# Differential heads' norm factors: one transposition to rows, a store to DRAM and four loads into all partitions, in place of sixteen transpositions

## The chip, the cores and the metric

The kernel runs on one core of a Trainium2 chip. The metric is the device time of one execution in microseconds (us), the median over the runs. TensorE is called PE in the profile, its weight loads PEld, VectorE DVE, ScalarE ACT, GpSimd POOL and SyncE SP.

## The reference, cut to what matters

Two transformer blocks on 512 tokens of width 1024. The change lies in the token mixer of the second block, which has four differential attention heads (width 128 each) and eight "fox" heads (width 64 each, with a forget gate). The differential heads end in a norm over each head's 128 features, per token:

```python
def rmsnorm(x, g):
    xf = x.astype(jnp.float32)
    y = xf * lax.rsqrt(jnp.mean(xf * xf, axis=-1, keepdims=True) + EPS)
    return (y * g.astype(jnp.float32)).astype(x.dtype)

    od = jnp.einsum('bhqk,bkhe->bqhe', ad.astype(dv.dtype), dv)
    od = rmsnorm(od, subln_g) * (1.0 - lambda_init)
    ...
    of = jnp.einsum('bhqk,bkhd->bqhd', pf.astype(fv.dtype), fv)
    return jnp.concatenate([od.reshape(B, Q_BLOCK, DIFF_WIDTH),
                            of.reshape(B, Q_BLOCK, FOX_WIDTH)], axis=-1)
```

So there is one factor for each of 4 heads x 512 tokens. The mixer's result goes through `w_out_2`.

## The kernel before, in words

Activations lie transposed: features in the 128 partitions, the 512 tokens along a row of 2 KB. Matrix products are made from three matmuls each (`three`, lines 903 to 907): every fp32 operand is split into a high and a low part, and high x high, high x low and low x high are summed in a bank of PSUM. The weights come as 198 slabs of 128 x 1024 (512 KB), in a fixed order (`PHASES`, lines 67 to 72), through two slots: SP loads slab n into `raw_slab` (`load_one`, line 752, after the low part of slab n-2), ScalarE makes the high part (`slab_hi`, line 1536; called with s it converts slab s+1, once TensorE has used slab s-1), VectorE the low part (`slab_lo`, line 2165). Each engine's instruction order is written out by hand, and semaphores hold the engines together. `plan_psum` (line 311) says for each use of a bank what the user before has to have finished.

The stages around the change, in TensorE's order:

- The "df" pass: the attention of the four differential heads. VectorE leaves each head's result in `kept[:, h]` (lines 2812 to 2819).
- The "fv" stage (lines 1402 to 1413): the values of the fox heads, 8 k-steps of 12 matmuls each over four slabs (two k to a slab). After k = 2 come `df_stats`, 16 small groups of matmuls with ones (32 instructions in all) that sum the squares of the four heads per token; after k = 4 come `df_spreads`, line 1396.
- The "fx" pass: 32 units of fox attention (8 heads x 4 query blocks), in steps that also hold pieces of the projections fq2, fk2, fq3, fk3 and of the output projection (`FILLS`, line 194). In each step: transpose the probabilities of an earlier unit, the scores of this unit, the values of an earlier unit, one piece of fill. VectorE does row maxima, normalising and the low parts of the transposed probabilities (`attention`, line 2326), ScalarE the exponentials and high parts (line 1624).

The norm factors before the change: ScalarE takes the root of the 16 columns of sums (line 2009), VectorE the reciprocal and a guard (lines 2238 and 2239), so `rstds` has 128 partitions (tokens of a tile) x 16 (head, tile). `df_spreads` waits for that (`rstd_done`) and makes for each head four transpositions of a column broadcast to 128 x 128 (`head_spread`, lines 1192 to 1198; its transposition is line 1197, which the first block's heads use too: 16 of the 32). The result is a 128 x 512 bank per head with the token's factor in every partition; the banks are 0, 1, 5 and 7 (`DF_SPREAD_BANKS`).

VectorE multiplies (`df_normed`, lines 2857 to 2859), ScalarE copies the high part (lines 2014 to 2016), VectorE makes the low part (`mix_low`, line 2586), and so on in turns through two buffers, heads 0 to 3 (lines 2861 to 2867). Behind this ScalarE converts a slab (line 2017), loads the table for the exponential (line 2018) and begins fx; VectorE does the low part of that slab (line 2868) and begins fx. In fx's step 0 ScalarE converts the slab of fk2, in step 1 it makes the first fox value's high part (line 2020, `fx_value_hi`) ahead of the first exponential (line 1671). TensorE's third score waits for the first exponential, since two banks are used in turns. The first pair of units reads the transposed probabilities `probsT` in step 6 (line 1076).

SP in this stretch: the slab loads, and after the slab of index fv + 4 the eight copies `fox_rows` (lines 779 to 784). POOL has two small copies in the stretch of fx and none in fv. In the first block POOL stores `decay_rows` to DRAM (line 847) and loads its four rows into all partitions (line 852).

Of the kernel before, what the change touches and what calls it, by code (L numbers as in the profile page):

```python
# [17 lines left out]
F32 = mybir.dt.float32  # L18
# [214 lines left out]
LAG_TAIL = {g: LAG_PV[g] + 1 for g in PASSES}  # L233
DF_SPREAD_BANKS = (0, 1, 5, 7)
CONVERT_AHEAD = {1: 7, 2: 8, 3: 9, 5: 10, 7: 11, 9: 12}
# [75 lines left out]
def plan_psum(sem):  # L311
# [4 lines left out]
    def use(key, bank, full, free, turns=1, step=0):  # L316
        uses[key] = (bank, freed.get(bank), full)
        freed[bank] = (free[0], free[1] + (turns - 1) * step)
# [108 lines left out]
    for t in range(ST):  # L427
        use(f"fv{t}", (2, 6, 3, 4)[t], slab("fv", 3), split(f"fv{t}"))
    for h in range(DF_H):
        filled = (sem.spread_ready, n + 1) if h == DF_H - 1 else (sem.df_spread, h + 1)  # L430
        use(("spread", f"df{h}"), DF_SPREAD_BANKS[h], filled, (sem.head_normed, ML_H + h + 1))
    attention("fx")
# [31 lines left out]
class Semaphores:  # L464


    def __init__(self, new):
# [106 lines left out]
        self.group_done = new("group_done")  # L574
        self.df_spread = new("df_spread")
        self.df_stat = new("df_stat")
# [7 lines left out]
def build(nc, xT, pT_in, pos_in, cols_in, square_in, onehot_in, relb_in, stream, out):  # L584
    scratch = nc.dram_tensor("bias_rows", [DF_H, S], F32, kind="Internal").ap()
    decay_rows = nc.dram_tensor("decay_rows", [ML_H, S], F32, kind="Internal").ap()
    with ExitStack() as ctx:
# [51 lines left out]
        fox_rows_set = [ctx.enter_context(nc.semaphore(f"fox_rows_set{h}")) for h in range(FX_H)]  # L639
        decay_loaded = [ctx.enter_context(nc.semaphore(f"decay_loaded{h}")) for h in range(ML_H)]  # L640
        x_loaded = [ctx.enter_context(nc.semaphore(f"x_loaded{k}")) for k in range(KD)]

# [252 lines left out]
        def _(pe):  # L895
# [295 lines left out]

            def head_spread(name, h, done):

                o = claim(("spread", f"{name}{h}"))
                for i in range(ST):
                    factor = rstds[:, RSTD0[name] + h, i:i + 1].to_broadcast([P, P])
                    last = pe.transpose(o[:, i * P:(i + 1) * P], factor, ident)
                last.then_inc(sem.spread_ready if h == 3 else done, 1)

# [19 lines left out]
            def first_fill(key, first, end):  # L1219

                if key in EXPANDED:
                    expansion(key)
                elif key == "mlstat":
                    head_stats("ml", lambda h: early[:, ML_SQ[h]], sem.ml_stat)
                elif key[:6] == "mlnorm":
                    if key == "mlnorm0":
                        pe.wait_ge(sem.rstd_done, NORM_NO["ml"] + 1)
                    head_spread("ml", int(key[6]), sem.ml_spread)
                elif key[:4] == "out1":
                    m = int(key[5])  # L1230
                    if first == 4:
                        claim(("out1", m, 0))
                        pe.wait_ge(sem.slab_lo, OUT1[m] + 1)
                    if (m, first) == (0, 4):
                        pe.wait_ge(sem.ml_lo, ML_H)
                    o = bank[uses[("out1", m, 0)][0]]
                    for k in range(first, end):
                        three(o[:, :], slab(0, out_slot(OUT1, m), k), pair(MIX_HI + k, MIX_LO + k), k == 4, False)
                else:
                    projection(key, first, end)  # L1240
# [154 lines left out]

            def df_spreads():

                pe.wait_ge(sem.rstd_done, NORM_NO["df"] + 1)
                for h in range(DF_H):
                    head_spread("df", h, sem.df_spread)  # L1400

            for n in range(KD // 2):
                slot = arrived("fv", n)
                for k in (2 * n, 2 * n + 1):
# [4 lines left out]
                    if k == 2:  # L1409
                        df_stats()  # L1410
                    elif k == 4:
                        df_spreads()
                last.then_inc(sem.slab_used, 1)
# [121 lines left out]
        def _(act):  # L1535
# [475 lines left out]
            nc.scalar.activation(forget_rows[0:FX_H, :], tiles[0:FX_H, PROB + 3], ACT.Copy)  # L2011
            operand_hi("ncum", forget_rows[HALF:HALF + FX_H, :], tiles[0:FX_H, PROB + 3])
            slab_hi(SLAB0["fv"] + 2)
            for h in range(DF_H):
                act.wait_ge(sem.head_normed, ML_H + h + 1)
                nc.scalar.activation(ar(MIX_HI + h), t(TMP + h % 2), ACT.Copy).then_inc(sem.mix_hi, 1)
            slab_hi(SLAB0["fv"] + 3)
            nc.scalar.activation(root_table[:, :], col("one"), ACT.Exp)
# [125 lines left out]
        def _(dve):  # L2144
# [710 lines left out]
            slab_lo(SLAB0["fv"] + 2)  # L2855

            def df_normed(h):
                factor = full(dve, ("spread", f"df{h}"))
                stt(t(TMP + h % 2), kept[:, h], sub_gain[:, 0:1], factor[:, :], ALU.mult, ALU.mult).then_inc(sem.head_normed, 1)

            df_normed(0)
            df_normed(1)
            for h in range(DF_H):
                mix_low(HEAD0["df"] + h, slice(0, P), h, t(TMP + h % 2))
                if h + 2 < DF_H:
                    dve.wait_ge(sem.mix_lo, HEAD0["df"] + h + 1)
                    df_normed(h + 2)
            slab_lo(SLAB0["fv"] + 3)
            def fx_value_lo(i):
# [296 lines left out]
```

## Time and profile before

| | |
|---|---|
| median of 3 runs | 1285.56 us (1285.51 to 1286.14) |
| the profiled execution | 1285.81 us |
| its span in the profile | 1284.0 us |
| granted clock of TensorE, mean | 0.998 of full |
| instructions | 17444 |
| DMA traffic | 120.98 MB, mean 94 GB/s |

The page gives the busy time of each engine as a share of the span. TensorE's matmuls are pipelined: a row's duration overlaps that of the next, and a timeline's starts show the pace. The fv stage runs from about 787.8 to 815.1 us of the span, the fx pass starts at 815.1.

### The profile page before, as it was taken

The page shows a single profiled execution, that of the slowest core. Times are in us where ns is not written, and L with a number is a line of the kernel's source. Part 1 is how long each engine was busy: PE and PEld are TensorE (multiplying, and loading weights), DVE is VectorE, ACT ScalarE, POOL GpSimd, SP SyncE. Part 2 cuts the span into 40 slices and gives each one's busy share as a digit, 9 for nine tenths or more (in the row PEclk, how much of TensorE's full clock was granted, in tenths as well). Part 3 has the DMA queues.
Part 4 walks back from the last instruction along what each step waited for, and adds up shares of the span by engine and source line. Part 5 has one row for each costly group of instructions (what it writes and reads, how often), then busy time and mean ns, then how long its engine had stood idle before and what let it go on. Part 6 is the DMA issues. An engine that isn't in the chain of part 4 may idle for free.

```text
span 1284.0 us, 17444 instructions
## 1 busy us (share of the span) xinstructions
PE 1270.1 (99%) x6386; PEld 1073.1 (84%) x6386; DVE 766.6 (60%) x1242; ACT 549.4 (43%) x920; POOL 43.3 (3%) x49
## 2 busy tenths in 40 slices
PE   9999999999999999999999999999999999999997
PEld 7888888988888888888888888888998888888886
DVE  6777895666444443323685896898868422455334
ACT  5646765443222223322564655667443222222221
POOL 4010000000000000000000000000000000000002
PEclk9999999999999999999999999999999999999999
DMA  5242013122333223332333322423122322223322
GB/s 199 83 131 82 34 34 129 36 70 96 98 98 98 94 91 126 99 114 98 99 94 119 99 83 87 119 74 116 50 66 84 113 90 93 96 98 98 99 99 82
DMA packets 37421, 120.98 MB, mean 94 GB/s; under 512 B 4585, under 2 KB 6761, under 8 KB 37361
## 3 DMA queue, kind: packets, MB, share of 16 engines
q1 hardware_dynamic: 35744, 116.93, 28.3%
q0 software_dynamic: 896, 2.64, 0.7%
q8 instruction: 39, 0.64, 0.2%
q10 hardware_dynamic: 720, 0.59, 0.1%
q14 instruction: 22, 0.17, 0.0%
HBM read 112.79 MB, written 2.11 MB: 89 GB/s over the span
## 4 chain that ended last, share of the span: by engine, by line
PE 95%; DVE 3%; ACT 1%; issue 1%; ACTq 0%; DVEq 0%
PE bank L905 29%; PE bank L906 29%; PE bank L907 29%; PE bank L1006 2%; PE bank L1099 1%; DVE arena L2157 1%; PE bank L1426 1%; PE bank L1144 1%; DVE tiles L2154 0%; PE bank L1128 0%; PE bank L1386 0%; PE bank L1385 0%; DVE w_lo L2154 0%; PE bank L1036 0%; DVE tiles L2157 0%
## 5 line engine op out<-in xcount | busy, mean ns | idle before, releaser
L2154 DVE TENSOR_TENSOR w_lo<-raw_slab,w_hi 128x1024 fp32r<-128x1024 f32 x198 | 243.7, 1231 | 269.1 <-ACT w_hi L1544 268.4
L905 PE MATMUL bank<-u_hi,w_hi 128*128 128x512 f32 x824 | 322.8, 392 | 0.0
L907 PE MATMUL bank<-u_hi,w_lo 128*128 128x512 f32 x824 | 321.0, 390 | 0.0
L906 PE MATMUL bank<-u_lo,w_hi 128*128 128x512 f32 x824 | 320.9, 389 | 0.0
L1544 ACT ACTIVATE w_hi<-raw_slab 128x1024 fp32r<-128x1024 f32 x198 | 208.8, 1055 | 185.3 <-PE bank L907 180.9
L905 PE MATMUL bank<-arena,w_hi 128*128 128x512 f32 (+1 forms) x692 | 261.1, 377 | 0.6 <-DVE w_lo L2154 0.6
L906 PE MATMUL bank<-arena,w_hi 128*128 128x512 f32 (+1 forms) x692 | 259.3, 375 | 0.0
L907 PE MATMUL bank<-arena,w_lo 128*128 128x512 f32 (+1 forms) x692 | 259.2, 375 | 0.0
L907 PEld LDWEIGHTS bank<-u_hi,w_lo 128*128 128x128 f32 x824 | 154.7, 188 | 32.4
L905 PEld LDWEIGHTS bank<-u_hi,w_hi 128*128 128x128 f32 x824 | 154.7, 188 | 31.7 <-issue 0.9
L906 PEld LDWEIGHTS bank<-u_lo,w_hi 128*128 128x128 f32 x824 | 154.8, 188 | 30.6
L905 PEld LDWEIGHTS bank<-arena,w_hi 128*128 128x128 f32 x692 | 130.3, 188 | 24.0 <-DVE w_lo L2154 1.2
L907 PEld LDWEIGHTS bank<-arena,w_lo 128*128 128x128 f32 x692 | 130.3, 188 | 23.6
L906 PEld LDWEIGHTS bank<-arena,w_hi 128*128 128x128 f32 x692 | 130.3, 188 | 21.9
L2154 DVE TENSOR_TENSOR tiles<-tiles 128x512 f32<-128x512 f32 (+3 forms) x122 | 81.9, 671 | 33.1 <-ACT tiles L1828 19.9
L2154 DVE TENSOR_TENSOR tiles<-bank,tiles 128x512 f32<-128x512 f32 (+2 forms) x75 | 51.3, 688 | 66.4 <-PE bank L907 63.5
L2154 DVE TENSOR_TENSOR arena<-tiles,arena 128x512 f32 (+3 forms) x88 | 59.1, 674 | 26.7 <-ACT arena L1875 20.5
L2103 ACT ACTIVATE arena<-tiles 128x512 f32 (+1 forms) x32 | 20.2, 630 | 100.2 <-DVE tiles L2154 100.2
L1671 ACT ACTIVATE tiles<-bank,negmax 128x128 f32<-128x128 f32 (+3 forms) x80 | 41.8, 525 | 36.7 <-DVE negmax L2377 35.5
L1875 ACT ACTIVATE arena<-tiles 128x512 f32 (+1 forms) x22 | 13.9, 632 | 83.2 <-DVE tiles L2154 83.2
L1651 ACT ACTIVATE probsT<-bank 128x128 fp32r<-128x128 f32 (+1 forms) x80 | 35.1, 438 | 24.9 <-PE bank L1099 24.6
L905 PE MATMUL bank<-u_hi,arena 128*128 128x256 f32 (+3 forms) x144 | 42.9, 298 | 0.8 <-DVE u_lo L2157 0.8
(274 smaller groups left out, 1466.8 us busy)
## 6 DMA issues: line engine op xcount, KB each, us to landing
raw_slab<-in_stream SPq DMA_DIRECT2D x198, 512.0 KB, 3.3
aside_raw<-in_stream SPq DMA_DIRECT2D x8, 512.0 KB, 5.2
arena<-arena SPq DMA_DIRECT2D x32, 128.0 KB, 2.3
residual<-in_xT SPq DMA_DIRECT2D x8, 256.0 KB, 6.9
out_hT<-residual SPq DMA_DIRECT2D x12, 128.0 KB, 1.7
arena<-forget_rows SPq DMA_DIRECT2D x8, 128.0 KB, 2.6
early<-decay_rows POOLq DMA_DIRECT2D x2, 256.0 KB, 4.1
arena<-decay_rows POOLq DMA_DIRECT2D x2, 256.0 KB, 5.8
```

What stands on the lines that cost most here:

```text
L905: pe.matmul(o, ws[0], xs[0], start=first, stop=False)
L906: pe.matmul(o, ws[0], xs[1], start=False, stop=False)
L907: return pe.matmul(o, ws[1], xs[0], start=False, stop=last)
L1006: return pe.matmul(o[:, c:c + P], square_, ones, start=first, stop=last)
L1099: last = pe.transpose(o[:, j * P:(j + 1) * P], tiles[:, src, j * P:(j + 1) * P], ident)
L1144: pe.matmul(bank[STAT_BANK][:, :], warm.to_broadcast([P, P]), warm.to_broadcast([P, S]), start=True, stop=True)
L1544: nc.scalar.activation(w_hi[:, s % 2], raw[:, s % 2], ACT.Copy).then_inc(sem.slab_hi, 1)
L1651: nc.scalar.activation(transposed(0, v % ST), by_key_tile(o, w), ACT.Copy).then_inc(sem.pT_hi, 1)
L1671: nc.scalar.activation(tiles[:, PROB + exp_slot(a, n, j), 0:w], o[:, 0:w], ACT.Exp, bias=negmax[:, e:e + 1], accum_out=rowsum[:, e:e + 1]) ...
L1875: nc.scalar.activation(arena[:, at(m, it, 2)], t(SQ + m), ACT.Copy).then_inc(sem.hidden_hi, 1)
L2103: nc.scalar.activation(arena[:, at(i, it, 2)], t(SQ + i), ACT.Copy).then_inc(sem.hidden_hi, 1)
L2154: return nc.vector.tensor_tensor(o, a, b, op)
```

## The change: what it does, and its diff

The sixteen transpositions of `df_spreads` are replaced by one of the whole 128 x 16 tile of factors, into 16 rows of bank 0 (row = head and token tile, 128 tokens each), after k = 3 instead of k = 4. ScalarE copies the rows to SBUF and stores them to a DRAM tensor of 4 x 512; when that store has landed it issues four loads, each of which puts one head's row of 512 factors into all 128 partitions of a tile `MO + h`. VectorE's `df_normed` reads the factors from there, after a wait for its head's load. The conversion of the slab after fv (high part on ScalarE, low part on VectorE) is moved ahead of the four heads' work on both engines. The head spreads of the first block stay as they are. Constants, semaphores and a rename are left out here:

```diff
-    for h in range(DF_H):
-        filled = (sem.spread_ready, n + 1) if h == DF_H - 1 else (sem.df_spread, h + 1)
-        use(("spread", f"df{h}"), DF_SPREAD_BANKS[h], filled, (sem.head_normed, ML_H + h + 1))
+    use("df_rows", DF_ROWS_BANK, (sem.spread_ready, n + 1), (sem.df_rows, 1))
...
+    factor_rows = nc.dram_tensor("factor_rows", [DF_H, S], F32, kind="Internal").ap()
...
-            def df_spreads():
-
+            def df_factor_rows():
+
+                o = claim("df_rows")
                 pe.wait_ge(sem.rstd_done, NORM_NO["df"] + 1)
-                for h in range(DF_H):
-                    head_spread("df", h, sem.df_spread)
+                every = rstds[:, RSTD0["df"]:RSTD0["df"] + DF_H].rearrange("p h n -> p (h n)")
+                pe.transpose(o[0:DF_H * ST, 0:P], every, ident).then_inc(sem.spread_ready, 1)
...
                     if k == 2:
                         df_stats()
-                    elif k == 4:
-                        df_spreads()
+                    elif k == 3:
+                        df_factor_rows()
...
             act.wait_ge(sem.forget_cum, 1)
             nc.scalar.activation(forget_rows[0:FX_H, :], tiles[0:FX_H, PROB + 3], ACT.Copy)
             operand_hi("ncum", forget_rows[HALF:HALF + FX_H, :], tiles[0:FX_H, PROB + 3])
+            rows = tiles[0:DF_H * ST, SQ, 0:P]
+            nc.scalar.activation(rows, full(act, "df_rows")[0:DF_H * ST, 0:P], ACT.Copy).then_inc(sem.df_rows, 1)
+            act.wait_ge(sem.df_rows, 1)
+            act.dma_start(factor_rows.rearrange("h (n p) -> (h n) p", p=P), rows).then_inc(sem.df_rows_stored, 16)
             slab_hi(SLAB0["fv"] + 2)
+            act.wait_ge(sem.df_rows_stored, 16)
+            for h in range(DF_H):
+                act.dma_start(t(MO + h), factor_rows[h].partition_broadcast(P)).then_inc(df_factor_loaded[h], 16)
+            slab_hi(SLAB0["fv"] + 3)
             for h in range(DF_H):
                 act.wait_ge(sem.head_normed, ML_H + h + 1)
                 nc.scalar.activation(ar(MIX_HI + h), t(TMP + h % 2), ACT.Copy).then_inc(sem.mix_hi, 1)
-            slab_hi(SLAB0["fv"] + 3)
             nc.scalar.activation(root_table[:, :], col("one"), ACT.Exp)
...
             slab_lo(SLAB0["fv"] + 2)
 
+            slab_lo(SLAB0["fv"] + 3)
+
             def df_normed(h):
-                factor = full(dve, ("spread", f"df{h}"))
-                stt(t(TMP + h % 2), kept[:, h], sub_gain[:, 0:1], factor[:, :], ALU.mult, ALU.mult).then_inc(sem.head_normed, 1)
+                dve.wait_ge(df_factor_loaded[h], 16)
+                stt(t(TMP + h % 2), kept[:, h], sub_gain[:, 0:1], t(MO + h), ALU.mult, ALU.mult).then_inc(sem.head_normed, 1)
 
             df_normed(0)
             df_normed(1)
...
                 if h + 2 < DF_H:
                     dve.wait_ge(sem.mix_lo, HEAD0["df"] + h + 1)
                     df_normed(h + 2)
-            slab_lo(SLAB0["fv"] + 3)
```

## Rows read from the trace of the kernel before

**Rows 1.** The page's busy times: engine, us (share of the span), instructions.
```profile
PE 1270.1 (99%) x6386; PEld 1073.1 (84%) x6386; DVE 766.6 (60%) x1242; ACT 549.4 (43%) x920; POOL 43.3 (3%) x49
```

**Rows 2.** The page's chain that ended last, shares by engine.
```profile
PE 95%; DVE 3%; ACT 1%; issue 1%; ACTq 0%; DVEq 0%
```

**Rows 3.** Line 1197, the spreads of all heads: ns min/median/max, first to last start.
```profile
L1197 PE MATMUL bank<-square,rstds x32: 270/272/291, 178.4 to 806.8; 128*128 128x128 f32 x32
```

**Rows 4.** TensorE's timeline, fv to fx: start us, us, line, count, [idle before <-releaser].
```profile
802.43 0.39 PE L905 MATMUL bank<-w_hi,u_hi 128*128 128x512 f32 x1
...
805.15 1.91 PE L1197 MATMUL bank<-square,rstds 128*128 128x128 f32 x16
806.82 0.47 PE L905 MATMUL bank<-w_hi,u_hi 128*128 128x512 f32 x1
807.13 0.39 PE L906 MATMUL bank<-w_lo,u_hi 128*128 128x512 f32 x1
...
815.09 0.33 PE L1426 MATMUL bank<-arena 128*128 128x128 f32 x2
```

**Rows 5.** ScalarE's timeline in the same stretch.
```profile
802.69 1.06 ACT L1544 ACTIVATE w_hi<-raw_slab 128x1024 fp32r<-128x1024 f32 x1 [0.39 <-PE bank L907]
...
810.12 0.63 ACT L2016 ACTIVATE arena<-tiles 128x512 fp32r<-128x512 f32 x1 [0.75 <-DVE tiles L2157]
...
811.73 1.28 ACT L2018 ACT_TABLE_LOAD   x1
813.02 0.20 ACT L2018 ACTIVATE small<-cols 128x1 f32<-128x1 f32 x1
815.34 1.06 ACT L1544 ACTIVATE w_hi<-raw_slab 128x1024 fp32r<-128x1024 f32 x1 [2.12 <-PE bank L907]
```

**Rows 6.** VectorE's timeline in the same stretch, and one row of step 6.
```profile
801.47 0.17 DVE L2157 SCALAR_TENSOR_TENSOR rstds<-rstds 128x16 f32<-128x16 f32 x1
...
805.79 1.41 DVE L2157 SCALAR_TENSOR_TENSOR tiles<-early,small,bank 128x512 f32<-128x512 f32 x2 [0.78 <-PE bank L1197]
...
811.74 1.23 DVE L2154 TENSOR_TENSOR w_lo<-raw_slab,w_hi 128x1024 fp32r<-128x1024 f32 x1 [0.26 <-ACT w_hi L1544]
...
829.49 0.42 DVE L2154 TENSOR_TENSOR probsT<-bank,probsT 128x256 fp32r<-128x256 f32 x1
```

**Rows 7.** TensorE's waits from 770 to 850 us (us, times, longest); the first one's row.
```profile
PE bank L1076 <- DVE probsT L2154: 0.6, 2, 0.5
...
830.06 0.35 PE L1076 MATMUL bank<-probsT,arena 128*128 128x256 f32 x1 [0.45 <-DVE probsT L2154]
```

**Rows 8.** DMAs through DRAM rows in the first block: issues, KB, us to landing.
```profile
early<-decay_rows POOLq DMA_DIRECT2D x2, 256.0 KB, 4.1
arena<-decay_rows POOLq DMA_DIRECT2D x2, 256.0 KB, 5.8
...
decay_rows<-tiles POOLq DMA_DIRECT2D x1, 8.0 KB, 1.8
bias_rows<-tiles POOLq DMA_DIRECT2D x1, 8.0 KB, 3.0
...
L852 POOL DMA_DIRECT2D early<-decay_rows x2: 541/559/577, 85.9 to 86.5; - x2
L852 POOL DMA_DIRECT2D arena<-decay_rows x2: 536/536/536, 87.0 to 87.5; - x2
...
DMA to landing us min/median/max: 3.5/5.0/6.1
```

**Rows 9.** DMA share by stretch (last but one), SP's fox copies, issues on ScalarE's queue.
```profile
807.00:809.00 2.00, 2.00 (x11) 1.62 (x10) 1.93 (x4) 1.09 (x3) 0.00 (x0) 1.00 0.89 204
809.00:811.00 2.00, 2.00 (x10) 1.66 (x9) 1.87 (x4) 1.25 (x3) 0.00 (x0) 1.00 0.96 214
...
803.75 5.62 SPq L784 DMA_DIRECT2D arena<-forget_rows  x8
...
L2139 ACTq DMA_DIRECT2D out_hT<-residual x4: 339/400/467, 1278.9 to 1281.8; - x4
```

More of the change, by code:

```diff
@@ L233 @@
 LAG_TAIL = {g: LAG_PV[g] + 1 for g in PASSES}
-DF_SPREAD_BANKS = (0, 1, 5, 7)
+DF_ROWS_BANK = 0
 CONVERT_AHEAD = {1: 7, 2: 8, 3: 9, 5: 10, 7: 11, 9: 12}
@@ L574, in __init__ @@
         self.group_done = new("group_done")
-        self.df_spread = new("df_spread")
+        self.df_rows = new("df_rows")
+        self.df_rows_stored = new("df_rows_stored")
         self.df_stat = new("df_stat")
@@ L640, in build @@
         decay_loaded = [ctx.enter_context(nc.semaphore(f"decay_loaded{h}")) for h in range(ML_H)]
+        df_factor_loaded = [ctx.enter_context(nc.semaphore(f"df_factor_loaded{h}")) for h in range(DF_H)]
         x_loaded = [ctx.enter_context(nc.semaphore(f"x_loaded{k}")) for k in range(KD)]
@@ L1190, in head_stats, with ml_spread @@
                     last.then_inc(sem.stat_ready if h == 3 else done, 1)
-            def head_spread(name, h, done):
-                o = claim(("spread", f"{name}{h}"))
+            def ml_spread(h):
+                o = claim(("spread", f"ml{h}"))
                 for i in range(ST):
-                    factor = rstds[:, RSTD0[name] + h, i:i + 1].to_broadcast([P, P])
+                    factor = rstds[:, RSTD0["ml"] + h, i:i + 1].to_broadcast([P, P])
                     last = pe.transpose(o[:, i * P:(i + 1) * P], factor, ident)
-                last.then_inc(sem.spread_ready if h == 3 else done, 1)
+                last.then_inc(sem.spread_ready if h == ML_H - 1 else sem.ml_spread, 1)
             def rank(n):
@@ L1227, in first_fill @@
                         pe.wait_ge(sem.rstd_done, NORM_NO["ml"] + 1)
-                    head_spread("ml", int(key[6]), sem.ml_spread)
+                    ml_spread(int(key[6]))
                 elif key[:4] == "out1":
```

## The prediction

> **What bounds the kernel now.** I began with the page's table of busy times: TensorE is busy for 1270.1 of 1284.0 us its weight loads included, and no other engine above 60% [rows 1]. The chain that ended last says the same: 95% of it is TensorE [rows 2]. So removed TensorE time looks like gain, and any gap the change opens on TensorE looks like loss. But a busy sum says nothing of the stage at hand, so I read next the engines' timelines around the sixteen transpositions, and the waits after them.
>
> Sixteen transpositions stand in the "fv" stage, at 805.15 us; the matmul after them starts at 806.82 [rows 4]. The row of their line gives a mean of 272 ns each [rows 3], which would make 4.35 us. That is the wrong price: matmuls overlap, and what counts is the distance between starts, (806.82 - 805.15)/16 = 0.104 us each.
>
> The one other place to look at is who is late behind this stage. TensorE waits for only 0.6 us between 770 and 850 us, twice, both times for VectorE's probsT; the first is 0.45 us at 830.06 [rows 7], right after VectorE's tile begun at 829.49 [rows 6]. So in the first steps of the "fx" pass VectorE, not TensorE, is what ends last. Followed back on VectorE's and ScalarE's timelines, that chain starts at ScalarE's conversion at 815.34, goes through the first fx value to VectorE and runs on there, nearly unbroken, to 829.9 [rows 5, 6]. In the kernel before, the conversion at 815.34 waits for TensorE's last fv matmul; ScalarE had been idle for 2.1 us, with the copies of the heads (last at 810.12) and the table load (811.73 to 813.01) long behind it [rows 5]. This is the slack the change spends.
>
> **The parts.** (a) TensorE: sixteen transpositions become one. Saved: 15 x 0.104 = 1.57 us. The one left has 16 output rows instead of 128; I take 0.104 us for it too (between 0 and the 0.27 us of its row [rows 3]).
>
> By the Trainium skill ("TensorE: Matmul & The Clock Gate", Part 4: PE-mode transpose), a transposition costs about 275 ns in a kernel's context. By that rule TensorE would save 15 x 0.275 = 4.1 us. The trace disagrees: starts are 104 ns apart, and 0.27 us is only the length of the overlapping row.
>
> (b) It now stands one k earlier, at 802.43 [rows 4]. It waits for the reciprocals, whose last instruction ends at 801.47 + 0.17 = 801.64 [rows 6]: no wait, 0.8 us of slack.
>
> (c) ScalarE gets a copy of 16 rows, a store and four loads. Copy at about 802.8 for 0.3 us. Its cover: the conversion that stood at 802.69 and waits for TensorE's second fv slab [rows 5] slips by the copy and one issue, 0.7 us. With VectorE's low part it is done by 805.9; its reader is TensorE's fourth fv slab at 808.05 (worked out in (e)), so the slip costs nothing. A DMA issue on ScalarE's queue takes 0.34 to 0.47 us [rows 9]; four take 1.6 us, in time in which ScalarE was idle.
>
> (d) The round trip through DRAM. No row shows this store from ScalarE; the nearest are the 8 KB stores of decay_rows, 1.8 us, and bias_rows, 3.0 us [rows 8]. I take 1.8 (the store goes out ahead of SP's copies for fox, which begin at 803.75 [rows 9]) and keep 3.0. Store issued 803.1, landed 804.9. The nearest for the four loads are the four broadcasts of decay_rows, same size: issued 85.9 to 87.5, landed after 3.5 to 6.1 us, medians 4.1 and 5.8 of the pairs [rows 8]. Counted from the first issue they land at +3.5, +5.3, +6.6 and +7.7 us. Here: 808.4, 810.2, 811.5, 812.6.
>
> (e) The moved conversion. The high and low parts of the slab after fv (for fq2) now stand ahead of the four heads' work on ScalarE and VectorE; they wait until TensorE has used the third fv slab. TensorE's next start after that slab is 802.43 + 0.10 + 0.08 (the first matmul behind a switch takes 807.13 - 806.82 = 0.31 instead of 2.72/12 = 0.23 [rows 4]) + 2 x 2.72 (one k, from 802.43 to 805.15 [rows 4]) = 808.05. ScalarE starts 0.25 us after such a start, as at 815.34 behind 815.09 [rows 4, 5]: 808.30. Then 1.06 us on ScalarE [rows 5], 0.04 to VectorE, 1.23 there [rows 6]. VectorE's first head can start at F = 810.6; before it started at 805.79 [rows 6]. Behind the moved wait on VectorE are all four heads, then everything of fx; on ScalarE the four head copies, the table load, and everything of fx. SP is touched as well: its next slab load waits for that low part, so it goes 2.4 us earlier, into the time of the factor loads. POOL's queue has nothing here.
>
> (f) From F on. Before, from the first head's start to the last head's copy took 810.12 - 805.79 = 4.33, plus 0.63 for the copy [rows 5, 6]; the operand moves from PSUM to SBUF, which I cost at nothing. Then table load and exponential, 811.73 to 813.22, 1.49 us, and some 0.06 of gaps [rows 5]. The conversion of 815.34 would start at F + 6.51 = 817.1, that is 1.8 us later than before. From there ScalarE and VectorE run as they did, all shifted by 1.8. TensorE, 1.57 us ahead when fx begins, meets this first at the third score (it waits for the first exponential) and fully at 830.06, where it waited for VectorE already. TensorE has no slack to win back behind that.
>
> **Sum.** The 1.57 us gained on TensorE are turned into waiting, and the end moves by +1.8 us: 1285.81 (this execution; its span is 1284.0, so 1.8 us lie around it) + 1.8 = 1287.6. The median is 0.25 us lower, which gives 1287.3. Each load that lands late adds to F: they are needed at F, F + 0.7, F + 2.2 and F + 3.55, so 810.6, 811.3, 812.8 and 814.15. The slacks are 2.2, 1.1, 1.3 and 1.5 us. The second load is the tight one; a few tenths of lateness are likelier than none, so I take 1287.6 against the median.
>
> A measurement of this kernel can tell about 0.2%, 2.6 us, from no change; 1287.6 is inside.
>
> **Rivals.**
> Late loads (slower). Place: VectorE's wait for the factors. The DMA engines are busy for 0.89 and 0.96 of 807 to 811 us [rows 9], with SP's eight copies for fox issued over 5.6 us from 803.75 [rows 9] and a slab. The four loads come on top. If half of that 3.7 us of work stands ahead of the second load, and the store takes 3.0, the second lands at 810.2 + 1.85 + 1.2 = 813.25, 1.95 us late: +3.8 in all, 1289.4. It decides once a load is over 0.8 us later than needed, 1.9 us behind my estimate. For it: the shares. Against it: the decay loads shared the engines with slabs too.
>
> The head work keeps its cover (slightly faster). If TensorE's wait behind 815 is not on ScalarE's order, the 1.57 us stay: 1284.0. The wait of 830.06 on VectorE speaks against it [rows 7].
>
> A dear table load. It is now on the chain. In the trace it takes 1.28 us and the exponential follows 0.01 us later [rows 5]. The Trainium skill ("ScalarE: Activation LUTs", What ACT_TABLE_LOAD costs) adds a drain of some 1.38 us to each. If such a drain now showed, 1287.3 + 1.4 = 1288.7. The trace shows no gap on either side of the load, so little for it.
>
> The change does more than I read on TensorE (say, full-length transpositions were the price: 15 x 0.27 = 4.1 us): 1281.5 if nothing else waited. The distance of the starts is against it.
>
> **Numbers.** Forecast (loads on time or up to 0.8 us late): 0.60, its own range 1287.0 to 1288.1. Late loads 0.27, table drain 0.04, gain kept 0.07, more removed 0.02. Slower by over 0.2%: 0.27 + 0.04 and 0.02 of the unforeseen, 0.33. Faster by over 0.2%: 0.02. Within: 0.65. The range goes from 1286.3 (part of the gain kept) to 1289.4 (late loads).
>
> **What would show it.** One transposition at about 802.4; ScalarE's conversion at about 808.3 and VectorE's first head near 810.6; if that head's wait is put down to a DMA rather than to its own engine, the loads are late. The conversion for fk2 starting near 817 instead of 815.3. TensorE idle by some 2 us at the third fx score, behind ScalarE, and by 1 to 2 us at the first probsT read. I am wrong if TensorE shows no new waits between 813 and 835 us, or if the stage behind fv starts later than 813.5, which would mean a wait inside fv itself.

## The result, and the profile after

The changed kernel is slower: a median of 1289.45 us (1288.92 to 1291.53, 7 runs) against 1285.98 (1285.31 to 1287.09, 7 runs), +3.47 us, a ratio of 1.0033 [1.0023, 1.0042]. I had predicted 1287.6 and a range from 1286.3 to 1289.4. What happened is the rival "late loads", which I had priced at 1289.4. The seven times fall into two groups, 1288.9 to 1289.5 four times and 1291.0 to 1291.5 three times; what sets them apart stayed open (runs 9 and 10). The profiled execution took 1289.07 with a span of 1287.3, 3.3 above the span before.

The page of after, busy times and the shares of the chain that ended last:

```profile
PE 1270.2 (99%) x6371; PEld 1072.4 (83%) x6371; DVE 767.4 (60%) x1242; ACT 549.5 (43%) x921; POOL 42.7 (3%) x49
...
PE 94%; DVE 2%; ACT 1%; DMA 1%; issue 1%; ACTq 0%; DVEq 0%
```

Fifteen matmuls are gone, yet TensorE's busy sum stands where it stood [rows 1]: what it saved it spent elsewhere (in matmuls at half clock, see the last section; in run 2, where the clock stayed full, the sum is 1268.7). And "DMA" is in the chain, where none was [rows 2].

TensorE's timeline of after (start, us, line, form, count, [idle before <-releaser]):

```profile
802.45 0.27 PE L1402 MATMUL bank<-square,rstds 128*16 128x128 f32 x1
802.48 0.47 PE L906 MATMUL bank<-w_hi,u_hi 128*128 128x512 f32 x1
...
813.48 0.33 PE L1428 MATMUL bank<-arena 128*128 128x128 f32 x2
...
816.70 0.40 PE L908 MATMUL bank<-u_hi,w_lo 128*128 128x512 f32 x1
820.65 0.61 PE L1428 MATMUL bank<-arena 128*128 128x384 f32 x2 [3.55 <-ACT tiles L1673]
```

TensorE kept its part: the transposition waits for nothing, and "fx" starts at 813.48 instead of 815.09 [rows 4], 1.61 us earlier (forecast 1.57). The third score then waits 3.55 us for ScalarE's first exponential.

ScalarE's timeline of after, same columns:

```profile
802.76 0.27 ACT L2016 ACTIVATE tiles<-bank 16x128 f32<-16x128 f32 x1 [0.43 <-PE bank L1402]
803.05 0.34 ACTq L2018 DMA_DIRECT2D factor_rows<-tiles  x1
...
806.13 1.97 ACTq L2022 DMA_DIRECT2D tiles<-factor_rows  x4
808.30 1.06 ACT L1546 ACTIVATE w_hi<-raw_slab 128x1024 fp32r<-128x1024 f32 x1 [3.75 <-PE bank L908]
...
816.58 0.63 ACT L2026 ACTIVATE arena<-tiles 128x512 fp32r<-128x512 f32 x1 [1.56 <-DVE tiles L2166]
817.23 1.28 ACT L2027 ACT_TABLE_LOAD   x1
818.53 0.20 ACT L2027 ACTIVATE small<-cols 128x1 f32<-128x1 f32 x1
818.64 1.04 ACT L1546 ACTIVATE w_hi<-raw_slab 128x1024 fp32r<-128x1024 f32 x1
```

The last row answers to 815.34 of before [rows 5]: 3.30 us later, and that is the whole rise of the span. The moved conversion starts at 808.30, as forecast. The store is issued at 803.05, but the loads only at 806.13.

VectorE's four heads in after:

```profile
810.54 0.75 DVE L2166 SCALAR_TENSOR_TENSOR tiles<-early,small,tiles 128x512 f32<-128x512 f32 x1
811.72 0.75 DVE L2166 SCALAR_TENSOR_TENSOR tiles<-early,small,tiles 128x512 f32<-128x512 f32 x1 [0.43 <-DMA tiles<-factor_rows]
...
813.60 0.75 DVE L2166 SCALAR_TENSOR_TENSOR tiles<-early,small,tiles 128x512 f32<-128x512 f32 x1 [0.53 <-DMA tiles<-factor_rows]
...
815.80 0.75 DVE L2166 SCALAR_TENSOR_TENSOR tiles<-early,small,tiles 128x512 f32<-128x512 f32 x1 [0.84 <-DMA tiles<-factor_rows]
```

The first head starts on time and names no DMA. The other three each wait for their factors, 1.8 us together, and the last starts at 815.80, where I needed it at 814.15, 1.65 us late. So the +3.3 splits in two: 1.65 from late loads and the other 1.65 from the new order (forecast 1.8). Runs 1 and 2 show the same halves.

The issues of the DMA view between 803 and 816 us (KB each, median us to landing), after:

```profile
arena<-forget_rows SPq DMA_DIRECT2D x8, 128.0 KB, 5.1
tiles<-factor_rows ACTq DMA_DIRECT2D x4, 256.0 KB, 5.8
raw_slab<-in_stream SPq DMA_DIRECT2D x2, 512.0 KB, 8.1
factor_rows<-tiles ACTq DMA_DIRECT2D x1, 8.0 KB, 3.1
```

and before:

```profile
arena<-forget_rows SPq DMA_DIRECT2D x8, 128.0 KB, 2.6
raw_slab<-in_stream SPq DMA_DIRECT2D x2, 512.0 KB, 3.5
```

All three streams slow each other: SP's copies for fox and its slabs take about twice as long to land as before. The second slab is also issued 2.3 us earlier than before (810.65 against 812.99), so the order alone could have a part in this; run 2 settles it.

### The profile page after: what moved, and what is told of

Same layout as the page of the kernel before. It is cut to its first block, busy times and chain, and to the rows that moved or that the text cites. A ratio compares the mean times of both kernels' runs of the same rounds, so it can differ in the third digit from the quotient of the medians.

```text
span 1287.3 us, 17420 instructions
## 1 busy us (share of the span) xinstructions
PE 1270.2 (99%) x6371; PEld 1072.4 (83%) x6371; DVE 767.4 (60%) x1242; ACT 549.5 (43%) x921; POOL 42.7 (3%) x49
## 3 DMA queue, kind: packets, MB, share of 16 engines
q10 hardware_dynamic: 1328, 1.65, 0.5%
## 4 chain that ended last, share of the span: by engine, by line
PE 94%; DVE 2%; ACT 1%; DMA 1%; issue 1%; ACTq 0%; DVEq 0%
PE bank L906 29%; PE bank L908 28%; PE bank L907 28%; PE bank L1007 2%; PE bank L1100 1%; PE bank L1428 1%; DMA tiles<-factor_rows 1%; PE bank L1145 0%; PE bank L1129 0%; DVE tiles L2163 0%; PE bank L1387 0%; DVE tiles L2166 0%; PE bank L1386 0%; PE bank L1037 0%; PE bank L1077 0%
```

## The experiments

**Theories.** A: two terms, the order of the work (+1.7) and late loads (+1.7). B: the loads cost it all and the order nothing. C: TensorE's saving is no saving. D: the table load on the path is what can be taken back. Later I added the clock: TensorE's granted clock falls after its new wait (in the expectations of runs 9 and 10 it is this that is called D). The stages ahead jitter: ScalarE's 16-row copy starts at 802.76 in after and between 802.3 and 803.9 in the other traces. So I line traces up by the start of that copy and call that "aligned". "After" is the trace of the changed kernel; each ratio is that of the medians to the kernel before, run beside it, with its 95% interval.

**1. Loads with the queues to themselves.** Six of SP's eight fox copies, and the slab load queued behind them, are held back until the factors are in.

```diff
                 if n == SLAB0["fv"] + 4:
-                    fox_rows()
+                    fox_rows(0, 2)
+                    sp.wait_ge(df_factor_loaded[DF_H - 1], 16)
+                elif n == SLAB0["fv"] + 6:
+                    fox_rows(2, FX_H)
```

> The changed kernel with the DMA queues kept quiet while the factors are loaded: SP issues two of its eight fox copies, then waits for the last factor load before it issues the next slab load, and the other six fox copies follow after the slab load behind that. Nothing is left out. Theory A (the end moved by two terms, 1.7 us for the moved conversion and 1.7 us for loads that land late, and the lateness is contention with SP's traffic): the loads land at +3.6, +5.3, +6.6 and +7.7 us of the first issue as in the first block, the waits of VectorE for the second to fourth head shrink from 1.8 us in sum to 0.3 or less, span 1285.7 to 1286.0 against 1287.3 of the changed kernel and 1284.0 of the one before. Rival R (the round trip is late by itself, its store at 3.1 us and its own 1 MB): the waits stay, span 1287.1 to 1287.5.

1287.58 us, +1.65, a ratio of 1.0013 [1.0004, 1.0023]. No head waits for a DMA. ScalarE's timeline:

```profile
815.72 0.63 ACT L2029 ACTIVATE arena<-tiles 128x512 fp32r<-128x512 f32 x1 [0.76 <-DVE tiles L2169]
...
817.77 1.04 ACT L1549 ACTIVATE w_hi<-raw_slab 128x1024 fp32r<-128x1024 f32 x1
```

The conversion stands at 817.77, aligned 816.94 (forecast 817.1), and the span of 1286.5, aligned 1285.6, is close to what theory A expected. Its DMA view says what the queues cost the loads:

```profile
tiles<-factor_rows ACTq DMA_DIRECT2D x4, 256.0 KB, 3.9
...
factor_rows<-tiles ACTq DMA_DIRECT2D x1, 8.0 KB, 3.0
```

The loads fall from 5.8 to 3.9 us, and rival R falls. The store stays at 3.0, but this run says little about it: the two fox copies that SP still issues are those beside the store, and they were beside it in after too. What held the store is in the part on the prediction, under (d).

**2. Factors loaded long before, from other data.** The store and the wait for it stay; the loads leave the path.

```diff
+            act.wait_ge(sem.operand_lo, SPLIT_NO["bias3"] + 1)
+            for h in range(DF_H):
+                act.dma_start(t(MO + h), decay_rows[h].partition_broadcast(P)).then_inc(df_factor_loaded[h], 16)
             slab_hi(SLAB0["fv"])
...
+            slab_hi(SLAB0["fv"] + 3)
             act.wait_ge(sem.df_rows_stored, 16)
-            for h in range(DF_H):
-                act.dma_start(t(MO + h), factor_rows[h].partition_broadcast(P)).then_inc(df_factor_loaded[h], 16)
-            slab_hi(SLAB0["fv"] + 3)
```

> The changed kernel with the four loads made some 20 us earlier, ahead of the fv stage, from the four rows that the first block stored (other data, so the heads' norm factors are not computed from this pass); the transposition, the copy and the store stay, and ScalarE waits for the store only after the moved conversion. No load can be late. Theory A: VectorE's first head starts at 810.5 as before, no waits between heads, the conversion for fk2 near 817.0, span 1285.6 to 1285.9 (+1.7, the price of the order alone). Rival B (all of the loss is the loads): the 1.57 us of TensorE show as gain, span 1282.4 to 1282.8.

1287.63, +1.70, 1.0015 [1.0006, 1.0025]. The conversion is at 816.71, aligned 817.0. The span of 1285.3, aligned 1285.6, is at the lower edge of what theory A expected. It agrees with run 1 by another road: without late loads the change costs 1.65 to 1.70. B falls: the order costs about 1.7, and by medians the loads cost 3.47 - 1.7, some 1.8 us (1.65 by the traces), so it isn't the order alone either. SP's transfers, in the changed order but without the four loads beside them:

```profile
arena<-forget_rows SPq DMA_DIRECT2D x8, 128.0 KB, 2.3
raw_slab<-in_stream SPq DMA_DIRECT2D x2, 512.0 KB, 4.1
```

So it is the four loads that stretch them to 5.1 and 8.1 us in after, and not the earlier slab.

**3. The kernel before, with the conversion moved and nothing else.**

```diff
             slab_hi(SLAB0["fv"] + 2)
+            slab_hi(SLAB0["fv"] + 3)
             for h in range(DF_H):
...
-            slab_hi(SLAB0["fv"] + 3)
```

(VectorE's slab_lo is moved alike.)

> The kernel before with all its sixteen transpositions, and only the conversion of the slab after fv moved ahead of the four heads on ScalarE and VectorE. Theory A: the conversion waits for TensorE's third fv slab, which ends 1.57 us later than in the changed kernel, so the first head starts at 812.1 instead of 805.8, the conversion for fk2 at 818.6 instead of 815.3, TensorE gets a wait of about 1.9 us or more at the third fx score; span 1287.1 to 1287.5, so +3.3 us without any DMA. Rival B (the order costs nothing, as TensorE's work covers it): 1283.8 to 1284.2.

1289.03, +3.10, 1.0024 [1.0014, 1.0034]. Its timelines, VectorE's heads:

```profile
811.10 1.23 DVE L2154 TENSOR_TENSOR w_lo<-raw_slab,w_hi 128x1024 fp32r<-128x1024 f32 x1 [5.99 <-ACT w_hi L1544]
812.25 1.40 DVE L2157 SCALAR_TENSOR_TENSOR tiles<-early,small,bank 128x512 f32<-128x512 f32 x2
```

The first head starts at 812.25 (expected 812.1). The order alone, with all sixteen transpositions kept, costs 3.1 us: with the conversion moved ahead of them, the heads wait for TensorE's third fv slab. This run adds no DMA to the kernel before, so B falls a second time. In the change itself TensorE's 1.6 us give half of that back.

**4. The kernel before, with four transpositions instead of sixteen,** one for each head.

```diff
-                for i in range(ST):
+                for i in range(ST if name == "ml" else 1):
```

(VectorE reads the one tile's 128 columns four times.)

> The kernel before with one transposition for each differential head instead of four, VectorE reading the same 128 columns four times (the factors of the first token tile are used for all four tiles). This is TensorE's gain alone, without the round trip and without the moved conversion. Theory A: 12 x 0.104 = 1.25 us are saved and stay saved, since the conversion at 815.3 starts when TensorE is done with fv; span 1282.6 to 1282.9. By the price of the row (0.27 us each) it would be 1280.8; if VectorE's chain does not depend on TensorE there, the gain is lost at the first read of probsT: 1283.5 to 1284.0.

1284.31, -1.62, 0.9987 [0.9978, 0.9997]. TensorE's row, against 805.15 and 1.91 [rows 4]:

```profile
805.37 0.60 PE L1197 MATMUL bank<-square,rstds 128*128 128x128 f32 x4
```

Twelve fewer bring 1.62 by medians and 1.1 by the spans of the two traces (1282.9 against 1284.0); 12 x 0.104 = 1.25 was expected. So where nothing new waits, the saving shows at the end, and C falls. It is no version to use, since all four token tiles get the first one's factors.

**5. The change with the conversion back behind the heads.**

```diff
-            slab_hi(SLAB0["fv"] + 3)
             for h in range(DF_H):
...
+            slab_hi(SLAB0["fv"] + 3)
```

> The changed kernel with the conversion of the slab after fv put back behind the four heads on both engines; the transposition, the store and the loads stay. Theory A (heads end when the last load allows, then everything behind them in order): the first head still waits for the first load (about 810), the last head's copy ends at 817.2 as in the changed kernel, the conversion for fq2 follows there, so the chain gets 1.06 us longer, and TensorE stands still from 813.6 to about 819.5 for the slab of fq2; span 1288.2 to 1288.6. If the heads end earlier without the 1.1 us of VectorE's moved work ahead of them, it is up to 0.5 us less. Rival B (the moved conversion was the loss, so undoing it gives it back): 1284.0 to 1285.6.

1292.17, +6.05, 1.0048 [1.0031, 1.0065]; the span of 1289.3 is 0.7 to 1.1 above what was expected. TensorE's timeline and a window of it (us; busy time of PE, PEld, DVE, ACT, POOL; granted clock, DMA share, GB/s):

```profile
819.72 0.77 PE L906 MATMUL bank<-u_hi,w_hi 128*128 128x512 f32 x1 [5.66 <-DVE w_lo L2163]
```

```profile
819.00:823.00 4.00, 3.28 (x10) 2.76 (x11) 1.56 (x4) 3.27 (x7) 0.00 (x0) 0.57 0.42 131
```

TensorE stands still for 5.66 us because the slab for its next stage is now last in the queue behind the late heads. So the move protects: without it the change would be dearer still. The miss is the clock: after the wait it is granted 0.57 until 823 (1.00 in the 3 us behind), and VectorE waits 0.8 us for the second score, which it never did before:

```profile
822.96 0.42 DVE L2386 TENSOR_REDUCE negmax<-bank 128x1 f32<-128x256 f32 x1 [0.82 <-PE bank L1430]
```

The six matmuls ahead of that score take 2.7 us here, from 819.72 to 822.41. At the 0.23 us between starts at full clock they would take 1.4 (an estimate), and VectorE would not have waited.

**6. The table load ahead of the heads,** where ScalarE is idle.

```diff
+            nc.scalar.activation(root_table[:, :], col("one"), ACT.Exp)
             for h in range(DF_H):
...
-            nc.scalar.activation(root_table[:, :], col("one"), ACT.Exp)
```

> The changed kernel with ScalarE's table load for the exponential (1.28 us, and the 0.2 us behind it) ahead of the four heads' copies, where ScalarE was idle for 1.96 us. Nothing is left out. Theory A (ScalarE's order behind the last head is on the chain): the conversion for fk2 starts at 817.2 instead of 818.6; span 1285.7 to 1286.1 against 1287.3. Rival C (VectorE alone sets it, behind its last head): the span stays at 1287.1 to 1287.5.

1289.09, +2.97, 1.0023 [1.0013, 1.0033]. The trace's span is 1288.1, some 2 us above what I expected; it is of an execution of 1289.93, 0.8 above the median. ScalarE's timeline, then the clock behind it and two rows of VectorE's timeline:

```profile
810.02 1.28 ACT L2024 ACT_TABLE_LOAD   x1
...
817.86 0.63 ACT L2027 ACTIVATE arena<-tiles 128x512 fp32r<-128x512 f32 x1 [2.04 <-DVE tiles L2166]
818.39 1.04 ACT L1546 ACTIVATE w_hi<-raw_slab 128x1024 fp32r<-128x1024 f32 x1
```

```profile
820.00:826.00 6.00, 5.59 (x15) 4.62 (x16) 5.59 (x12) 3.42 (x11) 0.00 (x0) 0.50 0.28 87
...
825.19 0.69 DVE L2386 TENSOR_REDUCE negmax<-bank 128x1 f32<-128x512 f32 x1 [0.30 <-PE bank L1430]
827.18 0.69 DVE L2163 TENSOR_TENSOR tiles<-bank,tiles 128x512 f32<-128x512 f32 x1 [0.64 <-PE bank L908]
```

The load itself did what it should: the conversion follows the last copy with nothing between. But in this execution the store took 3.6 us and the last head waited till 817.07 (the DMA waits are 2.4 us against 1.8), and TensorE ran at half clock, 1.2 GHz, for over 6 us. That is about twice as long as in after (last section), and TensorE's slack no longer hid it: VectorE waits for TensorE twice, 0.9 us together, which it doesn't do in after. So about 1 us of it reached the end: the span is 0.8 above that of after, though the conversion stands 0.25 earlier. The gain that I had expected was eaten in part by the later loads and in part by this. By medians the early table load alone brought 3.47 - 2.97 = 0.5 us.

**7. Both: quiet queues and the early table load.**

> Both mends at once: quiet DMA queues during the factor loads, and the table load ahead of the heads. Theory A: the conversion for fk2 starts at about 815.5, 0.2 us behind the kernel before; span 1284.1 to 1284.6, so the whole 3.3 us of loss are accounted for, and the 1.57 us of TensorE still do not show. Rival: the gain of TensorE shows now, 1282.4 to 1282.8.

1286.58, +0.46, 1.0002 [0.9992, 1.0011]: a tie with the kernel before, and a span (1284.0, aligned 1284.4) within the 1284.1 to 1284.6 expected. ScalarE's timeline:

```profile
815.33 1.06 ACT L1549 ACTIVATE w_hi<-raw_slab 128x1024 fp32r<-128x1024 f32 x1 [0.25 <-DMA raw_slab<-in_stream]
```

The granted clock is 1.00 from 820 to 824. The conversion is at 815.33, aligned 815.77, 0.4 after the one of before; it waits the last 0.25 us for its slab, which this version holds back. With 1.65 in run 1 and 0.46 here, the table load on the path was worth 1.2 us (by the traces 816.94 - 815.77, the same): D holds as a part, but doing away with it and with the late loads only gets back to the start. The 1.6 us of TensorE still don't show, since the heads start at 810.1 instead of 805.79 [rows 6].

**8. Another way to shorten the stage: the heads' sums one column wide,** in the kernel before.

```diff
-                        last = summed(o, h * ST + i, squares(h)[:, i * P:(i + 1) * P], True, True)
+                        pe.matmul(o[:, c:c + 1], square_, col("one"), start=True, stop=True)
```

> The kernel before, with the sixteen sums of the differential heads' squares written one column wide (a column of ones as the moving operand) instead of 128 columns of which one is read; nothing is left out. It shortens TensorE's fv stage without a round trip and without delaying the factors. The 32 instructions take 3.64 us now, 0.228 us for each of the sixteen sums. If the columns are the price, about 0.1 us each is saved, and the 1.6 us stay to the end: span 1282.2 to 1282.8. If the weight loads are the price, nothing is saved: 1283.8 to 1284.2. A saving that TensorE shows and the end does not would speak against theory A, which says that TensorE's time in fv is on the chain as long as ScalarE waits for it.

1288.2, +2.08, 1.0016 [1.0006, 1.0026]; the span of the trace is 1283.7. The 32 sums took

```profile
795.89 3.67 PE L1190 MATMUL bank<-cols,tiles 128*128 128x1 f32 x32
```

against 3.88 us for 128 columns each: 128 times less output, almost no time saved. Neither branch of the expectation covers the median: times ran from 1285.44 to 1290.08, and by and large with the mean granted clock, 0.998 in the two shortest and 0.995 in the four longest. Where the clock was lost wasn't seen, as the profile is of a short one, so the +2.08 has no shown cause.

**9. The change, unaltered, once more.**

> The changed kernel once more, unaltered, for the trace of another execution: seven executions gave 1288.9 to 1289.5 us four times and 1291.0 to 1291.5 three times. Theory D (a third term, TensorE's clock): after the wait at the third fx score the granted clock falls to half for some us; where that stretch ends within the slack that TensorE has until the first probsT read (1.85 us), the span is 1287.3, where it is longer the rest is added. A longer execution should then show the half clock for over 4 us after the wait, with no wait of TensorE at the probsT read, and no later loads. Rival E (the loads are later in the long executions): VectorE's last head starts over 1 us after 815.8 counted against the same start of the fx pass.

1290.67 (the kernel before, beside it, 1285.98), span 1288.9. The DMA waits are 2.3 us, not 1.8. Its clock:

```profile
818.00:823.00 5.00, 0.94 (x5) 0.72 (x5) 2.76 (x7) 4.57 (x8) 0.00 (x0) 1.00 0.23 90
823.00:826.80 3.80, 3.80 (x11) 2.98 (x11) 3.73 (x9) 2.27 (x6) 0.00 (x0) 0.56 0.42 137
```

Of the 1.6 us over the span of after, 1.1 were there at the copy already (803.87), and 0.5 are later loads. Half clock stood here for as long as in after, so it is not what makes one execution longer than the other, and what D asked for isn't there. Nor is that of rival E, loads over 1 us later: they are 0.5 later. Most of the difference arose in stages ahead of the change.

**10. TensorE kept busy in its wait:** 14 matmuls without a reader ahead of the third score.

```diff
+                if n == 2:
+                    for _ in range(14):
+                        pe.matmul(bank[5][:, :], u_hi[:, 0, 0:P], u_hi[:, 0], start=True, stop=True)
                 o = claim(("score", "fx", n, 0))
```

> The changed kernel with fourteen matmuls of 512 columns (3.2 us, results unused, in bank 5 before its next user) on TensorE ahead of the third fx score, where it stood still for 3.55 us. Nothing is left out. It changes what TensorE does while it would wait and nothing of the chain over the DMA, ScalarE and VectorE. Theory A plus D (D: a third term, TensorE's granted clock, which fell to half after the wait; where that outlasts the slack before the first probsT read, the rest is added): the clock stays at full, the span is 1287.1 to 1287.5 as with the wait, and the long executions (three of the changed kernel's seven, 1291.0 to 1291.5) vanish: all times within 1288.7 to 1290.0, median 1289.2. Rival E (later loads and the jitter of the stages before make the long executions, as in the second trace of the changed kernel, 1290.7 us): the spread from 1288.9 to 1291.5 stays. If TensorE's own time bound the stage, the 3.2 us would be added: 1292.5.

1289.52, +3.77, 1.003 [1.0018, 1.0041].

```profile
816.61 3.36 PE L1421 MATMUL bank<-u_hi 128*128 128x512 f32 x14
820.79 0.62 PE L1431 MATMUL bank<-arena 128*128 128x384 f32 x2 [0.82 <-ACT tiles L1676]
```

The clock stays at 1.00 in every window from 816 to 828 us, and the median is where it was, within 0.3 us of the expected 1289.2. So in the change as it is, half clock adds nothing to the median: it is hidden in slack that VectorE's lateness leaves. The 3.2 us of added matmuls cost nothing either. Its seven times lie between 1289.02 and 1290.28; of eight executions of the change four are above 1290.6. Whether that is the clock's doing these runs don't settle.

**11. Fox copies held back, the slab load not.**

```diff
                 if n == SLAB0["fv"] + 4:
-                    fox_rows()
+                    fox_rows(0, 2)
+                elif n == SLAB0["fv"] + 6:
+                    sp.wait_ge(df_factor_loaded[DF_H - 1], 16)
+                    fox_rows(2, FX_H)
```

> As the quiet queues, but only six of SP's eight fox copies are kept out of the factor loads' time; the slab load for fk2 is not held back and runs right after the first two copies. Theory A with the fox copies as the cause of lateness: loads on time within 0.3 us, span 1285.7 to 1286.2, median 1287.5 to 1288.0. If any 0.5 MB beside them makes them late, the waits of VectorE between heads sum to 0.8 us or more and the span is 1286.5 or more.

1288.45, +2.70, 1.0021 [1.0011, 1.0031], and a span of 1287.2, aligned 1286.3. I had expected a median of at most 1288.0 and loads on time; the other branch, waits between the heads of 0.8 us or more, didn't come either. Only the first head waits, 0.61 us. By medians holding back the six copies brings 3.47 - 2.70 = 0.8 us, and holding back the slab load too brings another 2.70 - 1.65 = 1.05. That is not a clean price of the slab: with the six copies out of the queue it goes out at 806.73 instead of 809.30, right beside the first load, and in this trace the store took 0.4 us longer than in run 1.

No version with all of the work done beats the kernel before.

## Why the prediction was right and wrong

**(a), (b) TensorE: right.** 1.61 us against 1.57. The one transposition shifts the next start by 0.03 us (802.45 to 802.48), less than the 0.104 I took. The price of 0.104 from the distance of starts held, and four transpositions in place of sixteen brought 1.62 at the end; 275 ns each would have brought 12 x 0.275 = 3.3.

**(c) ScalarE's copy and issues: right.** The four issues took 1.97 us instead of 1.6, in idle time, and the slipped conversion cost nothing: "fv" has no new wait.

**(d) The round trip: this step failed.** I took 1.8 us for the store, the lower of two rows, arguing that it goes out ahead of SP's copies. It took 3.06 in after and 2.9 to 3.6 in all nine traces that have it. That is 1.2 us or more of the slack of 1.1 to 2.2 us that I had left the loads. The DMA view shows why. It counts the packets that start in a window (packets, MB, share of the 16 DMA engines' time); the store is 16 packets of 512 bytes, each with a small one behind it, on queue q10. From 803.05 to 804.3, then from 805.0 to 805.15:

```profile
q8 instruction: 1, 0.02, 4.7%
q10 hardware_dynamic: 30, 0.01, 3.0%
...
q10 hardware_dynamic: 2, 0.00, 4.5%
```

Fifteen of the sixteen parts start within 1.2 us of the issue, and each reports some 0.35 us after its start. Nothing of q10 starts between 804.3 and 805.0. The last part starts at 805.01. The one packet of the queue "instruction", 16 KB, starts at 804.08 and takes 0.94 us (4.7% of 16 engines in 1.25 us), so it ends at 805.02. The same holds in run 6 (804.45 + 1.33 = 805.78, last part 805.76, store 3.6 us), in run 11 (804.79 + 1.46 = 806.25, last part 806.23, 3.4 us), and within 0.02 us in all nine. So I read that the last part stood behind this packet on its DMA engine. Its report comes 1.1 us after its start in all nine; why that takes longer than for the others, no view shows. No run moved the packet, so this cause is read from nine traces and not tested. No instruction of the kernel issues it, and it is in the kernel before as well, at 804.06, where I didn't look for it. I had thought only of SP's copies as company, and it was another. That the store came out near my upper bound of 3.0 is a coincidence.

Then I took the loads' times from decay_rows, with the last landing 7.7 us after the first issue; they were

```profile
L2022 ACTq DMA_DIRECT2D tiles<-factor_rows x4: 365/466/587, 806.1 to 807.5; - x4
...
DMA to landing us min/median/max: 3.7/5.8/7.8
```

Counted from the first issue they landed at +3.7, +5.6, +7.4 and +9.2 us, where I had taken +3.5, +5.3, +6.6 and +7.7. With the queues to themselves (run 1) it was +3.1, +4.2, +4.8 and +5.5, so the excess comes from what SP moves beside them. The last landed at about 815.35 instead of 812.6: 1.2 from the store and 1.5 from the loads, against 1.5 us of slack. Had the store taken my 1.8 us and the loads as long as they did, the last would have landed at 814.1, when it was needed at 814.15 (an estimate): each of the two mis-sized terms alone would have cost little, and both together cost the margin. The last head starts 0.45 us after that landing; the same 0.45 stands in runs 6, 9 and 10, and no view names what fills it.

And I named the second load as the tight one. The fourth was: under contention each load takes longer than the one before, so lateness adds up along the four (0.43, 0.53, 0.84), while I had spaced them by the decay loads' rows. The rival's arithmetic came to 1289.4 by 1.95 us on the second load alone. It hit the sum by luck, with the wrong load.

The Trainium skill ("DMA: Bandwidth & Descriptors", Anatomy of one DMA) gives about 2.0 us of fixed cost for a DMA that GpSimd issues, most of it the receipt of the write. This store goes out on ScalarE's queue, so the figure isn't one for it. In the trace fifteen of its parts reported within 1.5 us of the issue, under the page's figure, and only the sixteenth, at 3.06, above it.

The same page (Queues, rings and completion order) says that each DMA engine takes turns between the queues that have work for it. The landing times agree: the fox copies, issued as before, went from 2.6 to 5.1 us and the slabs from 3.5 to 8.1 beside ScalarE's four loads, and stood at 2.3 and 4.1 in run 2, without them.

**(e), (f) The order of the work: right.** 808.30 for the conversion (forecast 808.30), 810.54 for the first head (810.6), and with loads on time 816.9 and 817.0 (aligned) for the conversion behind the heads (817.1), a wait of 1.9 us at the third score, and +1.65 and +1.70 us at the end (+1.8). Slack that looked free on ScalarE, 2.1 us before 815.34 [rows 5], was what the move spent. That the path runs through this conversion is borne out by all the traces: in eleven of thirteen, of both kernels and of every run but 5 and 6, the span is the start of the conversion for fk2 plus 468.6 to 468.7 us (before 1284.0 and 815.34, run 4 1282.9 and 814.25, after 1287.3 and 818.64). In runs 5 and 6 it is 0.9 and 1.1 us more, where half clock made VectorE wait.

One sign did not come: the 1 to 2 us that I expected TensorE to wait at the first probsT read were 0.1 us in after and in run 1, and in run 2 0.45, as before. A part of TensorE's lead went in a wait of 0.7 us at a later score (run 2, 827.85), and in after and run 1 in matmuls at half clock, of which I had not thought.

**The other rivals.** "Gain kept" falls with runs 1 and 2: TensorE keeps its 1.6 us until the third score and loses them there. The table load shows no drain: 817.23 + 1.28 = 818.51, and the exponential starts at 818.53. "More removed" falls with (a).

**Chances.** I gave "late loads" 0.27. The argument against it, that the decay loads had shared the engines too, was weak: they shared them with slabs, these with slabs and eight copies, and the shares of 0.89 and 0.96 [rows 9] were there to be read. In after they are 1.07 and 1.08 from 809 to 813:

```profile
809.00:811.00 2.00, 2.00 (x11) 1.65 (x10) 1.61 (x2) 0.36 (x1) 0.00 (x0) 1.00 1.07 229
811.00:813.00 2.00, 2.00 (x10) 1.68 (x9) 1.56 (x3) 1.13 (x2) 0.00 (x0) 1.00 1.08 251
```

## What to carry to other kernels

A cut on the busiest engine pays only up to the next wait. Before pricing it, follow the engines that feed the stage behind it and see whose idle time the new order spends: here 1.6 us of TensorE were bought with a 3.1 us later start of the heads. A factor sent through DRAM costs its store, then its loads, each at the price it has among the transfers that are already under way: a DMA has landed only when the last of its parts has, so look at everything that is on the DMA engines when the store goes out, the packets of the instruction queue too, and where the engines are 0.9 busy, let lateness grow from load to load.

## What the runs showed of the hardware that I had not expected

**TensorE's clock after a wait.** In after the granted clock falls behind the wait of 3.55 us, and comes back:

```profile
817.00:820.60 3.60, 0.10 (x1) 0.00 (x0) 1.36 (x4) 3.57 (x8) 0.00 (x0) 1.00 0.25 99
...
821.60:825.30 3.70, 3.70 (x12) 2.92 (x11) 3.63 (x9) 2.19 (x6) 0.00 (x0) 0.54 0.45 142
825.30:828.00 2.70, 2.70 (x16) 2.18 (x15) 2.43 (x6) 1.88 (x6) 0.00 (x0) 1.00 0.00 0
```

Starts of full-width matmuls are 0.43 us apart at 822, against 0.23: the lower level, 1.2 GHz. The same came after 5.66 us (run 5), 3.1 (run 6), 4.06 (run 9) and 2.62 (run 11), and lasted some 3.4 us, in run 6 twice that. A wait of 1.85 us in run 1 lost the clock (0.55 from 821 to 824.8) and one of 1.92 us in run 2 did not. It cost about 1 us where VectorE then had to wait for TensorE (runs 5 and 6) and nothing elsewhere.

**A short store behind one packet.** The 8 KB store was done in about 1.5 us but for one of its sixteen parts, and that one came 1.4 to 2.1 us after the others in all nine traces, each time behind a 16 KB packet of the instruction queue (under (d)).

**Narrow matmuls save nothing behind a full weight load.** 32 sums of one column took 3.67 us, 0.115 each, against 0.121 for 128 columns. Each brings its own load of 128x128 weights, and I take that load to set the pace of both; that is argued from the unchanged time, and no run changed the weights.
